# Second network: attention steps handed out in lumps instead of one by one

## The chip, the cores and the metric

The kernel runs on one NeuronCore of a Trainium2 chip. The metric is the device time of one execution in microseconds. The engines work through their own queues in order and wait for each other on semaphores: TensorE (PE) does the matmuls, VectorE (DVE), ScalarE (ACT) and GpSimd (POOL) the rest, and SyncE (SP) issues the DMAs.

## The reference

Two networks of two layers each work one after the other on x of 256 rows and 1024 columns, in float32. The change lies in the second one. Each of its layers is a swiglu with a layer norm, then a mixing block with an output projection and a layer norm, and then a second swiglu with a layer norm. Cut to the mixing block:

```python
proj = x @ w_in[l]
(h_a, b_a, c_a, uv, q, kc, vc, ksl, vsl, kw, vw, gl) = jnp.split(proj, split_points, axis=-1)
y_a = short_conv(h_a, b_a, c_a, conv_w[l])
y_b = gmlp_spatial(uv, gmlp_ln_g[l], gmlp_ln_b[l], gmlp_w[l], gmlp_b[l])
y_c = nsa_attention(q, kc, vc, ksl, vsl, kw, vw, gl, ...)
mix = jnp.concatenate([y_a, y_b, y_c], axis=-1) @ w_out[l]
x = layer_norm(ALPHA * x + mix, ln2_g[l], ln2_b[l])
```

`nsa_attention` has 8 heads in two groups and three branches: attention to 15 compressed keys, to selected blocks (with 256 rows all four blocks are selected) and to a window (which covers all rows). The last two are thus plain causal attention over 256 rows with other keys and values. Each branch is weighted by a sigmoid gate and the three are summed.

## The kernel before, in words

The weights come in float32, 1 MB at a time (a unit), by DMA. ScalarE rounds a unit to fp32r (`high`, L1785), and VectorE forms the rest, weight less rounded weight, in two halves of 1024 columns (`low`, L2009). Each product is three matmuls of such parts (L217 to L219, or L224 to L226 where the result is added to a bank that holds the residual). Three units are held ready.

The whole program is written out by a planner in Python, `script`. It makes one list of steps; each engine then goes through the list in that order and issues its share of each step. The order of the list is therefore the order of every engine's queue. Where two pieces of work are mixed, one generator yields costs in microseconds for one of them and another for the other, and `mix(a, b, share)` (L248) takes steps of b until they cost `share` times what a has cost. A generator that can't go on yet yields `IDLE`; then mix goes on with a.

In the stage of the change, a is the rest of the projections, in 28 pieces of cost 1.44: four for the values (`lin_v`), four for the second half of the queries (`lin_q(1)`), eight for the convolution (`lin_conv`), four more (`lin_conv2`) and eight of the output projection (`lin_out`). Beside the last twelve, one step of `conv` is issued after each piece: gate, two tap steps, end, split. A unit belongs to each four pieces. Behind its second piece the conversion of the unit three ahead is queued on ScalarE, and behind the third and fourth piece one half each on VectorE (`spread`).

b is `nsa` (L1249), with a share of 1.04. It has eight tasks (`task`, L1284): key set 1 or 2, row half i = 0 or 1, and head pairs jp. Each task has four steps:

- scores: eight matmuls, a mask matmul on each of two banks, two maxima on VectorE (L2118), and exponentials on ScalarE (L1855)
- scale: reciprocal, gate and two multiplies of the probabilities on VectorE (L2146 to L2155). It has no TensorE work and a cost of 0
- turn: 4 or 8 transpositions (L1496), and a copy from PSUM for each of two banks, one on ScalarE and one on VectorE (L1863, L2125)
- values: 4 or 8 matmuls (L1638). After five sums of a row half, `o_split` copies the result as fp32r on ScalarE (L1795) and its rest on VectorE (L2021)

`slots(tasks, (-1, 0, -2, -1))` (L742) staggers them: slot n issues scale of task n-1, scores of task n, values of task n-2 and turn of task n-1, and yields each cost by itself, so that mix can put pieces between them. Behind each of them one step of a second chain, `side`, is issued and yielded by itself too: what is left of the gmlp block and of the key compression (`early`: gelu, mix, tanh, split), then for each row half the attention to the compressed keys (`compressed`: scores, max, exp, mask, turn L1751, values L1760). The second `compressed` waits for the convolution.

PSUM has eight banks, handed out in the order in which they were given back. In this stage one holds the running projection, two the sums of the values and, toward the end, four the output.

Of the kernel before, what the change touches and what calls it, by code (L numbers as in the profile page):

```python
# [27 lines left out]
PART = 1.44  # L28
# [200 lines left out]
def dense(banks):  # L229
    for b in banks:  # L230
        b.dense = True
    return banks


IDLE = "idle"
# [56 lines left out]
def chain(*gens):  # L292
    for g in gens:
        if callable(g):
            g = g() or ()
        yield from g


class Plan:
# [21 lines left out]
    def add(self, kind, *args):  # L321
        self.steps.append((kind, args))
# [128 lines left out]
def script(P):  # L451
# [274 lines left out]
    def score_pair(q, k, js, i, bias, mask, rs, q_events):  # L726

        bs, ers = [PB.take() for _ in range(2)], [ER.take() for _ in range(2)]
        K = 128 * (i + 1)
        if i:  # L730
            dense(bs)
        add("score_pair", bs, [[q[64 * hh:64 * hh + 64, j, i * 128:(i + 1) * 128] for hh in range(2)] for j in js],
            [[k(hh, j)[:, 0:K] for hh in range(2)] for j in js], mask, i, q_events)
        for hh in range(2):
            if bias is not None:
                add("biased", bs[hh], 2, K, bias(hh, js, K), ers[hh], P.small(2), rs[hh])
            else:
                add("soft", bs[hh], 2, K, P.small(2), ers[hh], rs[hh])
        PB.give(*bs)
        return ers  # L740

    def slots(tasks, order):  # L742

        for n in range(len(tasks) + 2):
            for x in order:
                if 0 <= n + x < len(tasks):
                    cost = next(tasks[n + x])
                    while cost is IDLE:
                        yield IDLE
                        cost = next(tasks[n + x])  # L750
                    if cost:
                        yield cost
                elif x == 0:
                    yield PART

    def turned(ers, i):

        K, T = 128 * (i + 1), i + 1
        ets = []
        for er in ers:  # L760
            tb, et = PB.take(), ET.take()
            add("weigh", tb, [er.ap[:, n * K + mt * 128:n * K + mt * 128 + 128] for n in range(2) for mt in range(T)], er, ("scaled", er.n), et, P.flip)
            P.flip = not P.flip
            PB.give(tb)
            ER.give(er)
            ets.append(et)
        return ets
# [90 lines left out]
    def first(l, o, now, nxt):  # L858
# [95 lines left out]
        def ca_attention():  # L954
# [8 lines left out]
            def task(i, jp):  # L963
                js, T = (2 * jp, 2 * jp + 1), i + 1
                rs, rc = P.small(4), P.small(4)
                ers = score_pair(q1, K, js, i, bias, None, [[rs[:, 2 * hh + n:2 * hh + n + 1] for n in range(2)] for hh in range(2)],
                                 [("q ca", l), ("k ca", l)])
                yield 1.45 + 0.95 * i
                add("scale", ers, rs, rc, None, 128 * T)
                yield 0  # L970
                ets = turned(ers, i)
                yield 0.44 * T
                if jp == 0:
                    obs[i], = dense([PB.take()])
                ob = obs[i]
                outs = [(hh, ob.ap[64 * hh:64 * hh + 64, j * 128:(j + 1) * 128], v1[:, mt, (2 * j + hh) * 64:(2 * j + hh + 1) * 64],
                         ets[hh].ap[:, (n * T + mt) * 128:(n * T + mt + 1) * 128]) for n, j in enumerate(js) for mt in range(T) for hh in range(2)]
                add("values_t", ob, ets, outs, jp == 0, jp == 1, [("v ca", l, 1)], [("ca read", l)] if i else [])
                ET.give(*ets)
                if jp == 1:  # L980
                    add("o_split", ob, range(4), (), (), [O2[:, z, 0:4, i * 128:(i + 1) * 128] for z in (0, 1)],
                        [("ht read", ("first", l - 1), 10)] if l else [], [("o2 ca", l)], 1.0)
                    PB.give(ob)
                yield 0.45 * T
# [105 lines left out]
    def second(l, o, nxt):  # L1090
# [158 lines left out]
        def nsa():  # L1249
            obs, sums = {}, [0, 0]  # L1250

            def part(i, kind, *args):

                if not sums[i]:
                    obs[i], = dense([PB.take()])
                ob = obs[i]
                add(kind, ob, *args[:2], sums[i] == 0, sums[i] == 4, *args[2:])
                sums[i] += 1
                if sums[i] == 5:
                    add("o_split", ob, range(4), (), (), [O1[:, z, 4:8, i * 128:(i + 1) * 128] for z in (0, 1)], [o1_before], [("o1 nsa", l, i)], 1.0 / ALPHA)  # L1260
                    PB.give(ob)

            def compressed(i):
                er, mx, rs = ER.take(), P.small(8), P.small(8)
                bs = [PB.take() for _ in range(2)]
                add("cmp_scores", l, i, bs, er, kcs)
                PB.give(*bs)
                yield 0.5
                add("cmp_max", l, i, er, mx)
                yield 0.5  # L1270
                add("cmp_exp", l, i, er)
                yield 0.5
                add("cmp_mask", l, i, er, rs, gts)
                yield 0.9
                tb, et = PB.take(), ET.take()
                add("cmp_turn", l, i, er, tb, et)
                PB.give(tb)
                ER.give(er)
                yield 0.3
                part(i, "cmp_values", l, et)  # L1280
                ET.give(et)
                yield 1.0

            def task(i, bno, jp):  # L1284

                js, T = (2 * jp, 2 * jp + 1), i + 1
                rs, rc = P.small(4), P.small(4)

                def K(hh, j):
                    return KS[64 * hh:64 * hh + 64, bno - 1, :]  # L1290
                if jp:
                    yield from at.until("q")
                ers = score_pair(Q, K, js, i, None, causalb, [[rs[:, 2 * hh + n:2 * hh + n + 1] for n in range(2)] for hh in range(2)],
                                 [("q nsa", l, jp), ("k nsa", l), "masks"])
                yield 1.1 + 0.5 * i
                gate = gts[:, 24 * i:24 * i + 24].rearrange("p (g j b) -> p g j b", g=2, j=4)[:, :, 2 * jp:2 * jp + 2, bno]
                add("scale", ers, rs, rc, (("gates", l), gate), 128 * T)
                yield 0
                ets = turned(ers, i)
                yield 0.44 * T  # L1300
                yield from at.until("v")
                outs = [(hh, lambda ob, hh=hh: ob.ap[64 * hh:64 * hh + 64, jp * 256:(jp + 1) * 256].rearrange("p (n q) -> p n q", n=2),
                         VS[:, mt, (bno - 1) * 128 + hh * 64:(bno - 1) * 128 + (hh + 1) * 64],
                         ets[hh].ap[:, 0:2 * T * 128].rearrange("p (n t q) -> p n t q", n=2, t=T)[:, :, mt, :]) for mt in range(T) for hh in range(2)]
                part(i, "values_t", ets, outs, [("v nsa", l)], [("win read", l)])
                ET.give(*ets)
                yield 0.45 * T
            main = slots([task(i, bno, jp) for jp in range(2) for i in range(2) for bno in (1, 2)], (-1, 0, -2, -1))
            side = chain(lambda: early, at.until("q"), lambda: compressed(0), at.until("conv"), lambda: compressed(1))
            for cost in main:  # L1310
                if cost is IDLE:
                    yield IDLE
                    continue
                yield cost
                x = next(side, IDLE)
                if x is not IDLE:
                    yield x
            yield from side

        at = Line()  # L1320
# [8 lines left out]
        early = weave([gmlp(0), gmlp(1), both()], 3)  # L1329
        mix(chain(lin_cmp(), lin_k(), lin_gates(), lin_q(0)), early, 0.6, False)  # L1330
        steps = nsa()
        acc = [[], []]

# [1052 lines left out]
def build(nc, I, out_ap):  # L2386
    with ExitStack() as ctx:
# [28 lines left out]
        sems = {k: ctx.enter_context(nc.semaphore("s_" + k)) for k in SEMS}  # L2416
        P = Plan(m, I)
        script(P)
        steps = P.settled()
        T = Events()  # L2420
# [41 lines left out]
```

## Time and profile before

| | us |
|---|---|
| median of 3 runs | 1994.32 (1994.09 to 1995.76) |
| the profiled execution | 1995.39 |
| its span | 1993.5 |
| TensorE busy | 1974.0 (99%), 13856 matmuls |
| VectorE busy | 1254.2 (63%) |
| ScalarE busy | 904.8 (45%) |
| GpSimd busy | 99.3 (5%) |
| DMA queue, share of 16 engines | 59.0% |

A busy TensorE isn't one at its peak: matmuls overlap, and the end of each is modelled. What counts is the distance between the starts. The granted clock of TensorE is full (1.00) over nearly the whole span. The stage of the change lies at about 1220 to 1295 us for the first layer and at 1716 to 1790 us for the second.

### The profile page before, as it was taken

What the parts mean: (1) busy time and instruction counts of PE and PEld (TensorE: products, weight loads), DVE (VectorE), ACT (ScalarE), POOL (GpSimd) and SP (SyncE); (2) the same over time, 40 slices, a digit from 0 to 9 for tenths busy, and PEclk for the clock granted to TensorE, in tenths of its full rate; (3) what the DMA queues carried; (4) which work ended last, traced back from release to release, by engine and by line L of the source; (5) the groups of instructions that cost most, each with busy time, mean ns of one, the idle gap of its engine ahead of it and who ended that gap; (6) DMA issues with size and microseconds to landing.
All of it is one profiled execution on the core that took longest, in us unless ns stands there. A gap on an engine that the chain in (4) does not pass through costs nothing.

```text
span 1993.5 us, 31852 instructions
## 1 busy us (share of the span) xinstructions
PE 1974.0 (99%) x13856; PEld 1801.5 (90%) x13856; DVE 1254.2 (63%) x1785; ACT 904.8 (45%) x1202; POOL 99.3 (5%) x84
## 2 busy tenths in 40 slices
PE   8999999999999999999999999999999999999998
PEld 7888999999888999999999989799999998979997
DVE  6566656665656766655565567765566556776555
ACT  4445444444445544444444445444444444444442
POOL 0000001000100000100100020010010002001000
PEclk9999999999999999999999999999999999999999
DMA  8444466666544455796666646368657665646663
GB/s 289 165 146 148 170 211 189 199 210 191 171 167 149 141 177 197 196 264 181 180 203 188 189 151 173 106 194 259 190 169 212 189 187 148 176 106 195 187 189 106
DMA packets 421412, 361.84 MB, mean 182 GB/s; under 512 B 29392, under 2 KB 361496, under 8 KB 421272
## 3 DMA queue, kind: packets, MB, share of 16 engines
q1 hardware_dynamic: 421272, 359.80, 59.0%
q8 instruction: 109, 1.79, 0.4%
q14 instruction: 31, 0.25, 0.0%
HBM read 358.72 MB, written 1.05 MB: 180 GB/s over the span
## 4 chain that ended last, share of the span: by engine, by line
PE 95%; DVE 4%; ACT 1%; issue 0%; DMA 0%; DVEq 0%; SPq 0%
PE ps L217 22%; PE ps L218 22%; PE ps L219 22%; PE ps L224 8%; PE ps L226 8%; PE ps L225 8%; PE ps L1496 2%; PE ps L1604 1%; DVE hl L2009 1%; PE ps L1638 1%; DVE small L2114 0%; PE ps L1609 0%; ACT hl L1785 0%; PE ps L1676 0%; DVE er L2112 0%; DVE er L2155 0%
## 5 line engine op out<-in xcount | busy, mean ns | idle before, releaser
L2009 DVE TENSOR_TENSOR hl<-raw,hl 128x1024 fp32r<-128x1024 f32 (+1 forms) x532 | 722.6, 1391 | 387.0 <-ACT hl L1785 385.9
L217 PE MATMUL ps<-xt,hl 128*128 128x256 f32 (+1 forms) x2672 | 754.2, 282 | 0.0
L218 PE MATMUL ps<-xt,hl 128*128 128x256 f32 (+1 forms) x2672 | 746.2, 279 | 0.0
L219 PE MATMUL ps<-xt,hl 128*128 128x256 f32 (+1 forms) x2672 | 745.8, 279 | 0.0
L1785 ACT ACTIVATE hl<-raw 128x2048 fp32r<-128x2048 f32 (+1 forms) x337 | 613.7, 1829 | 217.9 <-PE ps L226 157.5
L217 PEld LDWEIGHTS ps<-xt,hl 128*128 128x128 f32 (+1 forms) x2672 | 500.9, 187 | 5.4 <-issue 2.3
L218 PEld LDWEIGHTS ps<-xt,hl 128*128 128x128 f32 (+1 forms) x2672 | 501.1, 188 | 3.1
L219 PEld LDWEIGHTS ps<-xt,hl 128*128 128x128 f32 (+1 forms) x2672 | 500.8, 187 | 0.2
L224 PE MATMUL ps<-hl,o 128*128 128x512 f32 x656 | 261.3, 398 | 0.0
L226 PE MATMUL ps<-hl,o 128*128 128x512 f32 x656 | 259.0, 395 | 0.0
L225 PE MATMUL ps<-hl,o 128*128 128x512 f32 x656 | 258.8, 395 | 0.0
L217 PE MATMUL ps<-hl,xt 128*128 128x512 f32 (+1 forms) x576 | 207.7, 361 | 1.3 <-DVE hl L2009 1.3
L219 PE MATMUL ps<-hl,xt 128*128 128x512 f32 (+1 forms) x576 | 202.6, 352 | 0.0
L218 PE MATMUL ps<-hl,xt 128*128 128x512 f32 (+1 forms) x576 | 202.5, 352 | 0.0
L1833 ACT ACTIVATE th<-ps 128x256 f32<-128x256 f32 x132 | 50.6, 384 | 329.3 <-PE ps L219 329.3
L226 PEld LDWEIGHTS ps<-hl,o 128*128 128x128 f32 x656 | 123.5, 188 | 28.8
L224 PEld LDWEIGHTS ps<-hl,o 128*128 128x128 f32 x656 | 123.5, 188 | 27.3 <-issue 1.5
L225 PEld LDWEIGHTS ps<-hl,o 128*128 128x128 f32 x656 | 123.7, 189 | 25.5
L217 PEld LDWEIGHTS ps<-hl,xt 128*128 128x128 f32 x576 | 108.7, 189 | 19.2 <-DVE hl L2009 2.3
L219 PEld LDWEIGHTS ps<-hl,xt 128*128 128x128 f32 x576 | 108.6, 189 | 16.1
L218 PEld LDWEIGHTS ps<-hl,xt 128*128 128x128 f32 x576 | 108.9, 189 | 14.6
L2092 DVE SCALAR_TENSOR_TENSOR tm<-th,ps 128x256 f32<-128x256 f32 x132 | 55.5, 421 | 99.3 <-ACT th L1833 95.3
(197 smaller groups left out, 1578.9 us busy)
## 6 DMA issues: line engine op xcount, KB each, us to landing
raw<-in_w_in SPq DMA_DIRECT2D x83, 1024.0 KB, 5.0
raw<-in_w_ffn_in SPq DMA_DIRECT2D x88, 512.0 KB, 5.1
raw<-in_ffn_gate SPq DMA_DIRECT2D x88, 512.0 KB, 3.9
raw<-in_ffn_up SPq DMA_DIRECT2D x88, 512.0 KB, 5.2
raw<-in_ffn_down SPq DMA_DIRECT2D x44, 1024.0 KB, 5.1
raw<-in_w_ffn_out SPq DMA_DIRECT2D x22, 1024.0 KB, 5.0
raw<-in_w_out SPq DMA_DIRECT2D x24, 512.0 KB, 4.7
raw<-in_w_branch_a SPq DMA_DIRECT2D x8, 1024.0 KB, 5.0
```

Source lines behind the costliest of these rows:

```text
L217: e.matmul(out, l[0], r[0], start=start, stop=False)
L218: e.matmul(out, l[0], r[1], start=False, stop=False)
L219: return e.matmul(out, l[1], r[0], start=False, stop=stop)
L224: e.matmul(out, l[0], r[0], start=False, stop=True, skip_group_check=True)
L225: e.matmul(out, l[0], r[1], start=False, stop=True, skip_group_check=True)
L226: return e.matmul(out, l[1], r[0], start=False, stop=True, skip_group_check=True)
L1496: ins = e.transpose(b.ap[:, k * 128:(k + 1) * 128], x, ident)
L1604: ins = e.matmul(b.ap[:, n * K:(n + 1) * K], qs[n][hh], ks[n][hh], start=n == 0, stop=mask is None and n == 1)
L1785: e.activation(m["hl"][:, k % NHL, 0, c], m["raw"][:, k % NRAW, c], ACT.Copy).then_inc(s.high.up(*([("high", k, h)] if parts == 2 else [(" ...
L1833: e.activation(tha, ga, ACT.Tanh, scale=0.5).then_inc(done.up(th.full), 1)
L2009: e.tensor_tensor(lo[:, c], m["raw"][:, k % NRAW, 0:n][:, c], hi[:, c].bitcast(F), ALU.subtract).then_inc(s.low.up(("low", k), *([("low", ...
L2092: e.scalar_tensor_tensor(tma, tha, 1.0, ga, ALU.add, ALU.mult).then_inc(done.up(th.free), 1)
```

## The change

`slots` is replaced by a new function `lumps` in `nsa`. It goes through the same tasks in the same order, but adds the costs of a slot's steps up and yields them once. Mix can therefore place pieces only between slots. Where a task yields `IDLE`, what has been added up so far is yielded first. Behind each lump two steps of `side` are issued, and their cost is added to the lump's before it is yielded, where there was one step behind each attention step. Nothing is computed otherwise, and no instruction is added or left out.

```diff
+    def lumps(tasks, order):
+
+        for n in range(len(tasks) + 2):
+            lump = 0
+            for x in order:
+                if 0 <= n + x < len(tasks):
+                    cost = next(tasks[n + x])
+                    while cost is IDLE:
+                        if lump:
+                            yield lump
+                            lump = 0
+                        yield IDLE
+                        cost = next(tasks[n + x])
+                    lump += cost
+                elif x == 0:
+                    yield lump + PART
+                    lump = 0
+            if lump:
+                yield lump
...
-            main = slots([task(i, bno, jp) for jp in range(2) for i in range(2) for bno in (1, 2)], (-1, 0, -2, -1))
+            main = lumps([task(i, bno, jp) for jp in range(2) for i in range(2) for bno in (1, 2)], (-1, 0, -2, -1))
             side = chain(lambda: early, at.until("q"), lambda: compressed(0), at.until("conv"), lambda: compressed(1))
             for cost in main:
                 if cost is IDLE:
                     yield IDLE
                     continue
+                for _ in range(2):
+                    x = next(side, IDLE)
+                    if x is not IDLE:
+                        cost += x
                 yield cost
-                x = next(side, IDLE)
-                if x is not IDLE:
-                    yield x
             yield from side
```

## Rows read from the trace of the kernel before

**Rows 1.** Waits of TensorE over the span: who, for whom, us in total, times, longest.

```profile
PE ps L1638 <- DVE et L2125: 2.3, 2, 1.2
PE ps L1760 <- DVE et L2373: 1.6, 2, 0.8
PE ps L1496 <- DVE er L2155: 1.4, 2, 0.7
```

**Rows 2.** Busy us of each engine in the first layer's stage, clock, DMA share, GB/s.

```profile
1213.00:1300.00 87.00, 84.38 (x658) 70.67 (x654) 62.41 (x134) 41.33 (x100) 1.22 (x2) 1.00 0.46 132
```

**Rows 3.** Timeline of TensorE, a piece between steps: start, us, engine, line, what.

```profile
1232.03 0.36 PE L217 MATMUL ps<-xt,hl 128*128 128x256 f32 x1
1232.22 0.28 PE L218 MATMUL ps<-xt,hl 128*128 128x256 f32 x1
...
1234.80 0.27 PE L219 MATMUL ps<-xt,hl 128*128 128x256 f32 x1
1235.00 0.65 PE L1638 MATMUL ps<-et,v 128*64 128x256 f32 x4
```

**Rows 4.** Timeline of TensorE, steps of the first slots.

```profile
1222.78 0.39 PE L1609 MATMUL ps<-maskb 128*128 128x256 bf16 x2
1223.10 0.24 PE L1684 MATMUL ps<-cst,tm 30*128 30x30 f32 x2
1223.27 0.38 PE L217 MATMUL ps<-hl,xt 128*128 128x256 f32 x1
...
1227.18 1.00 PE L1733 MATMUL ps<-sg,v 128*128 128x64 f32 x8
1228.02 0.61 PE L1496 MATMUL ps<-cst,er 128*128 128x128 f32 x4
```

**Rows 5.** Timeline of ScalarE and VectorE around the first turn.

```profile
1225.37 1.93 ACT L1785 ACTIVATE hl<-raw 128x2048 fp32r<-128x2048 f32 x1
...
1226.01 0.76 DVE L2155 TENSOR_TENSOR er<-er,small 128x256 f32<-128x256 f32 x2
...
1227.35 1.22 DVE L2009 TENSOR_TENSOR hl<-raw,hl 128x1024 fp32r<-128x1024 f32 x1
1228.48 0.86 DVE L2338 SCALAR_TENSOR_TENSOR sg<-ps,small,sg 128x64 f32<-128x64 f32 x4
```

**Rows 6.** Timeline of VectorE, the last slots.

```profile
1268.64 1.29 DVE L2118 TENSOR_REDUCE small<-ps 128x2 f32<-128x512 f32 x2
...
1269.84 0.35 DVE L2294 TENSOR_SCALAR tm<-zb,small 128x256 f32<-128x256 f32 x1
...
1271.15 1.22 DVE L2009 TENSOR_TENSOR hl<-raw,hl 128x1024 fp32r<-128x1024 f32 x1
...
1272.86 0.69 DVE L2021 SCALAR_TENSOR_TENSOR o<-ps,o 128x512 fp32r<-128x512 f32 x1 [0.49 <-ACT o L1795]
...
1273.46 0.68 DVE L2125 COPY et<-ps 128x512 f32<-128x512 f32 x1
...
1276.50 0.17 DVE L2146 RECIPROCAL small<-small 128x4 f32<-128x4 f32 x1
...
1276.91 1.29 DVE L2155 TENSOR_TENSOR er<-er,small 128x512 f32<-128x512 f32 x2
```

**Rows 7.** Timeline of ScalarE, four exponentials of a task and a split.

```profile
1233.50 0.48 ACT L1855 ACTIVATE er<-ps,small 128x256 f32<-128x256 f32 x1 [2.82 <-DVE small L2118]
...
1235.32 0.26 ACT L1909 ACTIVATE small<-small 128x60 f32<-128x60 f32 x1
...
1237.26 0.39 ACT L1795 ACTIVATE o<-ps 128x256 fp32r<-128x256 f32 x1
```

**Rows 8.** TensorE's first full and last matmuls, and the last clock change (columns as rows 2).

```profile
10.82 0.63 PE L218 MATMUL ps<-hl,xt 128*128 128x512 f32 x1
...
1986.43 0.39 PE L226 MATMUL ps<-hl,o 128*128 128x512 f32 x1
...
1989.50:1990.00 0.50, 0.00 (x0) 0.00 (x0) 0.40 (x2) 0.00 (x0) 0.00 (x0) 0.70 0.00 0
```

## The prediction

> **What bounds the kernel now.** I read the page's shares first (the table above): TensorE is busy 1974.0 of 1993.5 us, so almost every microsecond is either matmul work or the step from one matmul to the next, and an edit that only reorders can save no more than idle time and the cost of changing from one kind of work to another. Then the waits of TensorE: apart from the start there are three kinds, each with two occurrences, one per layer of the second network, 5.3 us together [rows 1]. All lie in the stage that the diff touches: 84.38 of 87 us busy, so 2.6 us idle per layer [rows 2]. Last the timeline of that stage, engine by engine, to see what each later queue is doing when TensorE arrives.
>
> **The order before and after.** Both follow from the costs in the code: `mix` hands out attention steps until they have cost 1.04 times what the projection pieces (1.44 each) have. Adding this up by hand for 28 pieces, the old order comes out as the trace shows it. The new one, with t0 to t7 for the tasks: lump n holds scale t(n-1), scores t(n), values t(n-2), turn t(n-1), then two side steps. The lumps 0 to 8 stand behind pieces 1, 3, 5, 7, 10, 12, 15, 18 and 20, lump 9 is cut in two behind 22 and 23, and the last compressed pair stands behind 25, as before. (Lump 8 is cut too, but both parts fall behind piece 20.) The pieces begin again behind attention work 12 times, where it was 23.
>
> **What is removed: 11 re-entries.** The first matmul of a piece takes 0.19 us to the second, against 0.117 between later ones, and work on 64 rows begins 0.20 behind the last one [rows 3]: 0.08 going in and 0.08 coming out, 0.16 for each, 1.8 us per layer. Something comes back: a score pair ends in a bf16 mask matmul, behind which an fp32 instruction starts only 0.32 later [rows 4], where a piece starts after 0.15. Seven lumps now have fp32 work there: 7 x 0.17 = 1.2 us, if the row, which is for a small transposition, holds for values and turns too. So between 0.6 and 1.8; I take the middle, -1.2 us per layer.
>
> **What is added: waits inside the lumps.** The turn of t(n-1) needs its rows scaled by VectorE. In the old order pieces stood between scores, values and turn; now they don't, while VectorE and ScalarE still have the same things queued, in particular the conversions of the weights (ScalarE 1.93 us, then VectorE in halves of 1.13) [rows 5]. I walk each lump with the durations of the rows.
>
> Lump 1: piece 2 starts 0.84 us later than the old 1223.27, because a mix of eight matmuls moves ahead of it [rows 4]; pieces 2 and 3 take 2.98, scores 0.97. TensorE is at the turn of t0 at 1228.06. ScalarE's conversion still starts at 1225.37 and lasts 1.93, so VectorE's first half still starts at 1227.35 and gives it free at 1228.48. In the old order the scaling of t0 was done before it, at 1226.01 [rows 5]; now it is queued behind it, as it comes behind piece 3. With 0.41 for the reciprocal and the small multiply [rows 6] and 0.42 for the first scaled tile (the pair is recorded with 0.76) the turn can start at 1229.3: a wait of 1.25, and 0.1 for the second tile. Price 1.35.
>
> Lump 3: from the end of the scores of t2 TensorE has values 0.58, a turn 0.44, two splits 0.5, two pieces 2.98, scores 1.39, values 0.58: 6.5 us. The other chain: maximum 0.7, four exponentials 1.82 [rows 7], a copy and two splits at some 0.4 [rows 7], a conversion 1.93, VectorE's half 1.13, scaling 0.41 + 0.69: 7.85. Price 1.35, and 0.15 for the second tile: 1.5.
>
> Lump 6: the turn of the compressed probabilities and their product are the two side steps of one lump, with no piece between. That is the place where the old order waits 0.8 us at its end [rows 1]; the first of the two pairs was covered by a piece. VectorE is some 0.25 later here, since maximum and copy of two tasks are queued first. Price 1.05.
>
> Lump 8, the largest. VectorE in the old order needed 1276.91 + 0.69 (its time for 128x512) - 1268.64 = 9.0 us from the first maximum of t7 to its first scaled tile [rows 6], and TensorE waited 1.2 and 0.7. New queue, from that same maximum: two maxima 1.2; then the low half of `o_split`, which used to stand behind a tap step and a conversion. It can't start before ScalarE has finished four exponentials (0.7 + 1.82) and its own half (128x512; by the 0.39 for 256 and 1.93 for 2048 columns I estimate 0.61): 3.2. From there split 0.6, copy 0.6, taps 1.3, conversion 1.13, taps 1.3, conversion 1.13, scaling 0.41 + 0.69: 10.4 us. TensorE's cover in the same time: values 0.58, turn 0.86, pieces 19 and 20 2.98, values 1.01: 5.4, since piece 21 now stands behind the turn. A wait of 5.0 and 0.15 for the second tile, where there were 1.9 before: +3.3.
>
> Elsewhere the walk leaves room: the turns of lumps 2, 4, 5, 6 and 7 find their tiles scaled 0.8 to 2.5 us before, the banks of the new order are free when taken (nearest: the compressed scores, in lump 4, take a bank whose exponential ends 0.6 us before), and rings, loads and units are asked for at the same pieces as before. The last pair waits 0.8 as before. The DMAs aren't moved; of SP's and POOL's queues nothing is passed.
>
> **Sum** per layer: 1.35 + 1.5 + 1.05 + 3.3 = 7.2, less 1.2: +6.0 us. The two layers have the same steps, and the waits come in twos [rows 1]: +12.0. What follows is paced by TensorE, so nothing is won back. The profiled run took 1995.4 with a span of 1993.5, 1.1 above the median 1994.3; the difference is added to the median: 2006.3. With each wait 0.5 us shorter and the switches at 1.8 it is 2001, with each 0.5 longer and the switches at 0.6 it is 2011.5.
>
> **Rules of the skill.** TensorE's granted clock is 1.00 in this stage [rows 2], so nothing can be won on it. The Trainium skill (Perfetto Trace Analysis, Matmul Optimizations) says that it is "important that matmuls execute back-to-back in batches", because the engine scales with its use; that speaks for lumps, and would give a gain only if the clock were low somewhere.
>
> **Rivals.**
> *A. The clock falls in the long wait.* At the kernel's end the last matmul starts at 1986.43, and between 1989.5 and 1990 the granted clock is 0.70 on average, a change from the upper level (2.4 GHz) to the lower (1.2 GHz) some 3 us after the last matmul [rows 8]. The new 5 us wait is longer. The first matmuls of the kernel, after a 5.3 us wait, are recorded with 0.63 us [rows 8] where full speed gives 0.40, for about seven of them and 16 transposes before. Price: 7 x 0.2 for the matmuls alone, up to 3.2 with the transposes, for each fall; both layers give 2009 to 2012.5. The Trainium skill (TensorE: Matmul & The Clock Gate, Part 1: The HAM clock gate) says the same: an idle engine is throttled, and activity releases it.
> *B. Only the tail pays.* If VectorE is a microsecond ahead of my walk in lumps 1, 3 and 6, three waits go: +3.3 - 1.2 = 2.1 per layer, 1998.5. For it: VectorE is busy only 62.4 of 87 us in the stage [rows 2]. Against: the conversion sets its time, not its load.
> *C. Faster.* One mechanism: the queue in front of t7's scaling. If the `o_split` half and the taps overlap with ScalarE so that the scaled tile comes within 7 us of the first maximum, the wait there falls to the old 1.9, and if the other lumps are covered as in B, the 11 re-entries remain: -1.8 per layer, 1990.7. It decides at 5.4 + 1.9 us; the rows put it at 10.4, and in the old order at 9.0.
> *D. The lumps are no lumps.* Where a task or the side yields idle, a lump is cut. By the costs this happens in 8 and 9 only. If it happened everywhere, the time would be as before, within 0.2%.
>
> **Chances.** Forecast 0.50 (2001 to 2009), A 0.20 (2007 to 2012.5), B 0.15, C 0.07, D and other things that cancel 0.08. A measurement can tell about 0.2% (4 us) from no change: faster 0.07; within 0.2%, D and a third of B, 0.13; slower 0.80. The range, 1998.5 to 2012, holds the forecast, A and most of B.
>
> **What would show it.** Of the changed kernel: TensorE's waits in this stage should have turns waiting for the scaled tile three times per layer (about 1.3, 1.4 and 5.0), and the product of the compressed probabilities twice (about 1.1 and 0.8); busy time of the stage longer by some 6 us at equal work; 12 re-entries of the 0.32 or 0.20 kind in place of 23. ScalarE's half of `o_split` should come straight behind t7's exponentials with VectorE idle before the low half. If the long wait is under 3 us, the tail's walk is wrong; if matmuls behind it are recorded with over 0.28 us for 256 columns, A holds; if lumps 1 and 3 don't wait, B does.

## The result and the profile after

The changed kernel takes 2012.96 us (median of 5 runs, 2011.57 to 2013.64) where the kernel before takes 1994.32: a ratio of 1.0089 with an interval of 1.0078 to 1.0099, or 18.6 us more. The sign was forecast; the size was not, and the time lies above the range. The profiled execution took 2013.23 us with a span of 2011.4.

The page of the kernel after: busy time of the engines, and the shares of the chain that ended last.

```profile
PE 1979.2 (98%) x13856; PEld 1804.0 (90%) x13856; DVE 1255.1 (62%) x1785; ACT 904.7 (45%) x1202; POOL 99.4 (5%) x84
...
PE 92%; DVE 5%; ACT 2%; issue 1%; DMA 0%; DVEq 0%; SPq 0%
```

The same 13856 matmuls, as they must be. The kernel before had 95% of its chain on TensorE and 4% on VectorE. So the new time lies in waits for VectorE, and TensorE's busy time has risen too, by 5.2 us at equal work. Those are two effects, and the forecast had only the first.

All lines behind `slots` are moved by 21: the turn is L1517 (was L1496), the values L1659, the mask L1630, scale L2167 to L2176, the conversion L1806 on ScalarE and L2030 on VectorE. Waits of TensorE in the kernel after over the whole span (who, for whom, us in total, times, longest):

```profile
PE ps L1517 <- DVE er L2176: 14.2, 6, 4.7
PE ps L1781 <- DVE et L2394: 3.6, 4, 1.0
```

Beside [rows 1]: the wait of the values has fallen from 1.2 to 0.1 us, turns wait three times per layer in place of once, and the compressed product waits twice in place of once. Timeline of TensorE in the first layer (start, us, engine, line, what; in brackets the idle time before it), the two early turns:

```profile
1229.54 0.64 PE L1517 MATMUL ps<-cst,er 128*128 128x128 f32 x3 [1.21 <-DVE er L2176]
...
1242.94 1.26 PE L1517 MATMUL ps<-cst,er 128*128 128x128 f32 x8 [1.17 <-DVE er L2176]
```

And the tail of the same layer, VectorE, ScalarE and TensorE together:

```profile
1273.13 1.29 DVE L2139 TENSOR_REDUCE small<-ps 128x2 f32<-128x512 f32 x2 [1.77 <-PE ps L1630]
...
1275.67 0.61 ACT L1816 ACTIVATE o<-ps 128x512 fp32r<-128x512 f32 x1
...
1276.31 0.69 DVE L2042 SCALAR_TENSOR_TENSOR o<-ps,o 128x512 fp32r<-128x512 f32 x1 [1.89 <-ACT o L1816]
...
1277.75 1.08 PE L1659 MATMUL ps<-et,v 128*64 128x256 f32 x8
...
1278.82 1.22 DVE L2030 TENSOR_TENSOR hl<-raw,hl 128x1024 fp32r<-128x1024 f32 x1
...
1281.26 1.22 DVE L2030 TENSOR_TENSOR hl<-raw,hl 128x1024 fp32r<-128x1024 f32 x1
...
1282.80 1.29 DVE L2176 TENSOR_TENSOR er<-er,small 128x512 f32<-128x512 f32 x2
...
1283.55 1.97 PE L1517 MATMUL ps<-cst,er 128*128 128x128 f32 x8 [4.71 <-DVE er L2176]
1285.17 0.78 PE L224 MATMUL ps<-hl,o 128*128 128x512 f32 x1
1285.74 0.63 PE L225 MATMUL ps<-hl,o 128*128 128x512 f32 x1
1286.17 0.63 PE L226 MATMUL ps<-hl,o 128*128 128x512 f32 x1
...
1287.20 0.40 PE L226 MATMUL ps<-hl,o 128*128 128x512 f32 x1
```

This is the queue of the forecast, item by item: maxima at 1273.13, the low half of `o_split` after 1.89 us of idle VectorE, two tap steps with a conversion behind each, then the scaling of t7. The first scaled tile is done 10.4 us after the first maximum (1282.80 + 0.69 - 1273.13). Behind the wait, the eight transpositions are recorded with 1.97 us where the turn at 1242.94 took 1.26, and matmuls of 512 columns start 0.43 apart and are recorded with 0.63, until the spacing is 0.23 and the record 0.40 again.

Busy time of each engine around the two long waits of the kernel after (columns as rows 2: PE, weight load, DVE, ACT, POOL, granted clock, DMA share, GB/s):

```profile
1281.00:1283.00 2.00, 0.00 (x0) 0.00 (x0) 1.93 (x5) 0.00 (x0) 0.00 (x0) 1.00 0.00 0
1283.00:1285.00 2.00, 1.46 (x7) 1.46 (x8) 1.09 (x2) 0.30 (x1) 0.00 (x0) 0.62 0.59 169
1285.00:1287.00 2.00, 2.00 (x8) 1.66 (x7) 1.28 (x2) 0.43 (x2) 0.00 (x0) 0.52 1.18 317
1287.00:1289.00 2.00, 2.00 (x11) 1.37 (x9) 0.69 (x1) 2.00 (x2) 0.00 (x0) 1.00 0.16 38
...
1788.00:1790.00 2.00, 2.00 (x10) 1.90 (x9) 0.54 (x2) 0.60 (x1) 0.00 (x0) 0.50 1.07 312
1790.00:1792.00 2.00, 2.00 (x7) 1.52 (x6) 1.30 (x3) 1.06 (x2) 0.00 (x0) 0.50 0.76 195
```

The clock falls from the upper level (2.4 GHz) to the lower (1.2 GHz): rival A's case. In the first layer it falls as the wait ends, at about 1283.5, and is back up at about 1287. In the second it falls at about 1785.3, in the middle of a wait that ends at 1787.62, and stays low for nearly 7 us, until 1792; some 4.5 us of that are work.

**Where the 18.6 us are.** From the first piece of the stage to the first transposition of the layer norm that ends it, the kernel before needs 82.27 us in both layers, the kernel after 90.85 and 91.37: 8.58 + 9.10 = 17.7 us, of 17.9 by which the spans of the two profiled executions differ. The remaining 0.9 is within the spread of the runs of either. Net of TensorE's recorded waits (2.63 us per layer before, 8.87 and 8.84 after) the stage takes 79.64 before and 81.98 and 82.52 after. These two numbers, *waits* and *net*, are the measure for all that follows. Waits under 0.15 us are not counted and stay in the net time, and so does what a low clock costs.

### The profile page after: what moved, and what is told of

It reads as the page before. It is cut to its first block, busy times and chain, and to the rows that moved or that the text cites. A ratio compares the mean times of both kernels' runs of the same rounds, so it can differ in the third digit from the quotient of the medians.

```text
span 2011.4 us, 31840 instructions
## 1 busy us (share of the span) xinstructions
PE 1979.2 (98%) x13856; PEld 1804.0 (90%) x13856; DVE 1255.1 (62%) x1785; ACT 904.7 (45%) x1202; POOL 99.4 (5%) x84
## 3 DMA queue, kind: packets, MB, share of 16 engines
HBM read 358.72 MB, written 1.05 MB: 179 GB/s over the span
## 4 chain that ended last, share of the span: by engine, by line
PE 92%; DVE 5%; ACT 2%; issue 1%; DMA 0%; DVEq 0%; SPq 0%
PE ps L217 21%; PE ps L218 21%; PE ps L219 21%; PE ps L224 8%; PE ps L226 8%; PE ps L225 8%; PE ps L1517 2%; DVE hl L2030 1%; ACT hl L1806 1%; PE ps L1625 1%; ACT er L1876 1%; PE ps L1659 1%; DVE er L2176 0%; DVE small L2135 0%; PE ps L1697 0%
## 5 line engine op out<-in xcount | busy, mean ns | idle before, releaser
L2030 DVE TENSOR_TENSOR hl<-raw,hl 128x1024 fp32r<-128x1024 f32 (+1 forms) x532 | 722.4, 1390 | 389.4 <-ACT hl L1806 388.4
L1806 ACT ACTIVATE hl<-raw 128x2048 fp32r<-128x2048 f32 (+1 forms) x337 | 613.8, 1829 | 222.5 <-PE ps L226 159.0
```

Source lines behind the costliest of these rows:

```text
L1806: e.activation(m["hl"][:, k % NHL, 0, c], m["raw"][:, k % NRAW, c], ACT.Copy).then_inc(s.high.up(*([("high", k, h)] if parts == 2 else [(" ...
L2030: e.tensor_tensor(lo[:, c], m["raw"][:, k % NRAW, 0:n][:, c], hi[:, c].bitcast(F), ALU.subtract).then_inc(s.low.up(("low", k), *([("low", ...
```

## The experiments

Where an expectation names a theory by a letter, K is the one with the clock's fall in it, and Q the one that puts the waits down to the order of VectorE's queue. The kernel before had 1995.78, 1994.67 and 1995.13 us on the chips of the experiments. "Entries" are the places where pieces begin again behind other work. The net time of e2 holds some 4.1 us of added work. Chips differ by up to 1.5 us, so differences between runs of different chips are taken from the stages of their traces.

| kernel | us | ratio to before | interval | first layer: length | waits | net | entries |
|---|---|---|---|---|---|---|---|
| before | 1994.32 | 1 | | 82.27 | 2.63 | 79.64 | 23 |
| after | 2012.96 | 1.0089 | 1.0078 to 1.0099 | 90.85 | 8.87 | 81.98 | 12 |
| e1 | 2003.31 | 1.0043 | 1.0030 to 1.0055 | 86.65 | 6.00 | 80.65 | 14 |
| e2 | 2009.73 | 1.0070 | 1.0056 to 1.0084 | 89.45 | 4.81 | 84.64 | 12 |
| e3 | 2010.01 | 1.0072 | 1.0059 to 1.0085 | 89.42 | 7.59 | 81.83 | 12 |
| e4 | 2015.52 | 1.0099 | 1.0086 to 1.0113 | 92.26 | 8.77 | 83.49 | 11 |
| e6 | 1999.14 | 1.0020 | 1.0011 to 1.0030 | 84.12 | 3.63 | 80.49 | 14 |
| e7 | 2005.75 | 1.0056 | 1.0042 to 1.0070 | 87.28 | 6.48 | 80.80 | 18 |
| e8 | 1994.12 | 0.9996 | 0.9987 to 1.0004 | 81.55 | 1.47 | 80.08 | 23 |
| e9 | 1991.78 | 0.9986 | 0.9977 to 0.9994 | 80.49 | 0.68 | 79.81 | 24 |
| e10 | 2022.96 | 1.0138 | 1.0122 to 1.0154 | 98.20 | 11.60 | 86.60 | 12 |
| e11 | 1993.95 | 0.9995 | 0.9986 to 1.0004 | 82.00 | 1.67 | 80.33 | 15 |
| e12 | 1992.12 | 0.9983 | 0.9974 to 0.9992 | 80.49 | 0.69 | 79.80 | 24 |

### The tail alone: e1_tail_apart

From slot 7 on the steps are handed out one by one, as the kernel before does; slots 0 to 6 stay lumps.

```diff
+            if n == 7:
+                P.apart = True
+            if P.apart:
+                for x in order:
+                    ...
+                        if cost:
+                            yield cost
+                    ...
+                continue
```

> The changed kernel, but from slot 7 on the steps are handed out one by one, as before. Theory K: of the 18.6 us some 3.6 are two falls of the TensorE clock behind the 4.7 us waits for the scaled tiles of t7, 6 are those waits themselves, and the rest are the waits in lumps 1, 3 and 6 with nothing won by fewer re-entries. Then the tail waits are 1.2 and 0.7 again, the clock stays at 1.00, and the time is 2013.0 - 3.6 - 2 x 3.0 = 2003.4. Rival R: a lower clock costs nothing here and the excess over my sum lies in the lumps themselves; then only the waits go, 2007.

Measured 2003.31. The two stages are shorter than in the kernel after by 4.20 and 4.72 us, 8.9 together (the medians, of two chips, differ by 9.65). So half of the loss lay in the tail, the clock's share with it. The waits of t0, t2 and the first compressed product are still there (1.2, 1.2 and 1.0), the clock is 1.00 throughout the stage. With the waits taken off, the stage is still 1.0 us longer than before although pieces begin again 9 times less. That is the first sign that the 1.2 us for the re-entries are not there.

### The clock alone: e2_warm

In front of t7's turn TensorE does 36 transpositions of the identity into the bank that the turn then fills, so that it is busy in the long wait, with nothing else changed.

```diff
+        for _ in range(warm):
+            e.transpose(tb.ap[:, 0:128], ident, ident)
```

> The changed kernel with 36 extra transpositions of the identity on TensorE (0.105 us each, 3.8 us) into the bank that t7's turn takes, placed in the 4.7 us wait; their result is overwritten. K: the turn starts at the same time, but the clock doesn't fall: 2013.0 - 3.6 = 2009.4, the first layer shorter by 1.5 and the second by 2.1. R: 2013 or a little more.

Timeline and window of e2_warm, first layer:

```profile
1278.69 4.15 PE L1638 MATMUL ps<-cst 128*128 128x128 f32 x36
...
1283.48 1.26 PE L1518 MATMUL ps<-cst,er 128*128 128x128 f32 x8 [0.64 <-DVE er L2179]
1284.49 0.48 PE L224 MATMUL ps<-hl,o 128*128 128x512 f32 x1
...
1283.00:1287.00 4.00, 3.52 (x19) 2.90 (x20) 2.55 (x5) 1.51 (x3) 0.00 (x0) 1.00 0.86 239
```

The turn starts where it did (1283.48 against 1283.55), since VectorE sets it. But the clock is 1.00, the turn takes 1.26 again instead of 1.97, and the stage is shorter by 1.40 us in the first layer and 1.90 in the second. So the fall costs 3.3 us, worked out as two stages; the medians say 3.2. In the first layer 0.61 of the 1.40 lie in the eight transpositions (1.62 against 1.01 to the next start) and 0.79 in the twelve matmuls behind them (3.76 against 2.97); in the second it is 0.61 and 1.28, since the clock comes back later. It is the measured price of rival A. It also separates two effects of one wait: the turn came no earlier, and the kernel was faster all the same.

### Taking one item out of VectorE's queue: e3_split_late

The first `o_split` is issued behind the second tap step instead of in front of t7's copy.

```diff
-                    add("o_split", ob, range(4), ...)
-                    PB.give(ob)
+                    def split(ob=ob):
+                        add("o_split", ob, range(4), ...)
+                        PB.give(ob)
+                    ...
+                if c:
+                    comp["split"]()
```

> The changed kernel, but the first o_split is issued behind the second tap step, so that VectorE doesn't stand idle for ScalarE's half (1.9 us in the changed kernel). If the order of VectorE's queue sets the long wait, it shrinks from 4.7 to about 3.4: -2.6 us in all, and -3.6 more if the clock then stays: 2006.8, or up to 2010.4 if it falls in both layers. If only the missing TensorE cover sets it, it stays 4.7 and the time 2013.

Waits of TensorE in e3_split_late over the span, and one window of it:

```profile
PE ps L1524 <- DVE er L2183: 11.6, 6, 3.4
...
1281.00:1283.00 2.00, 2.00 (x10) 1.76 (x10) 0.79 (x2) 0.60 (x1) 0.00 (x0) 0.53 0.92 271
```

The wait fell from 4.71 to 3.4, as forecast from the durations of the queue: it is the sum of what stands in front of the scaling (Q). The clock fell all the same in both layers, so 3.4 us of idle TensorE were enough here.

### Covering the wait with pieces: e4_piece_back

Lump 8 is cut in front of t7's turn, so that pieces 21 and 22 stand before it.

```diff
+                    if n == 8 and x == -2:
+                        yield lump + PART
+                        lump = 0
```

> The changed kernel, but lump 8 is cut between the values of t6 and the turn of t7, so that pieces 21 and 22 stand between them (3.0 us of cover, VectorE's queue as in the changed kernel up to t7's scaling). K: the wait falls to 1.7, the clock stays: 2013.0 - 6.2 - 3.6 + 0.4 = 2003.6. R: 2007.2.

It missed by 12 us: 2015.52. Waits, timeline of ScalarE and TensorE, and windows of e4_piece_back:

```profile
PE ps L1520 <- DVE er L2179: 8.2, 6, 1.7
PE ps L1768 <- ACT et L1887: 5.8, 2, 2.9
...
1285.31 1.89 ACT L1809 ACTIVATE hl<-raw 128x2048 fp32r<-128x2048 f32 x1
...
1287.11 0.58 ACT L1887 ACTIVATE et<-ps 128x512 f32<-128x512 f32 x1
...
1285.00:1287.00 2.00, 0.00 (x0) 0.00 (x0) 1.29 (x2) 2.00 (x2) 0.00 (x0) 0.97 1.17 321
1287.00:1289.00 2.00, 1.26 (x12) 1.26 (x14) 0.00 (x0) 1.70 (x4) 0.00 (x0) 0.50 0.28 67
...
1291.00:1293.00 2.00, 2.00 (x6) 1.60 (x5) 1.90 (x7) 0.00 (x0) 0.00 (x0) 0.50 0.00 0
```

The wait for the scaled tile is 1.7, as forecast. But a new one of 2.89 us stands behind it: the compressed scores take the bank of t7's turn, and ScalarE's copy of that bank (1287.11) is queued behind a weight conversion (1285.31, 1.89 us). I had walked VectorE's queue and not ScalarE's. The other lesson is the clock: no single wait is over 2.9 us, and yet it goes from 1.00 to 0.50 at about 1287 and stays there until after 1293. It falls 2.0 us into the wait of 2.9; the wait of 1.7 had ended 1.25 us before that one began (1283.60, and 1284.85). The waits of 1.2 in the same stage brought none. What the two waits each contribute was not taken apart.

### The early waits: e6_low_late

e1, and VectorE's two conversion halves are queued one piece later each.

```diff
+        self.let_low()
+        if self.late and piece in (2, 3):
+            self.held = piece
+            return
...
+    def let_low(self):
+        if self.held is not None:
+            self.add("need_low", self.held - 2)
+        self.held = None
```

> The kernel of e1 (lumps up to slot 6, the tail one by one), but VectorE's two halves of each weight conversion are queued one piece later, so that in lumps 1 and 3 the scaling stands ahead of the half. Theory Q (the place of the conversion in VectorE's queue makes the waits of 1.2 us in these lumps): both go, -6.0 us against e1, ratio 1.0013 to the kernel before. Rival D (VectorE is loaded too much when TensorE comes in lumps, wherever the conversion stands): at least half of the two waits stays, ratio 1.003 or more.

Waits of TensorE in e6_low_late in its first layer (1213 to 1310), and the timeline of the first scaling and the first turn:

```profile
PE ps L1815 <- DVE et L2428: 1.8, 2, 1.0
PE ps L1693 <- DVE et L2180: 1.1, 1, 1.1
PE ps L1551 <- DVE er L2210: 0.7, 1, 0.7
...
1225.56 0.76 DVE L2210 TENSOR_TENSOR er<-er,small 128x256 f32<-128x256 f32 x2
...
1226.99 0.39 PE L1664 MATMUL ps<-maskb 128*128 128x256 bf16 x2
1227.22 0.60 PE L1551 MATMUL ps<-cst,er 128*128 128x128 f32 x4
```

Both early waits are gone: the scaling of t0 is done before the conversion (1225.56; 1228.97 in the kernel after), and the turn follows the mask without a stop. (Its stage begins 0.95 us earlier than that of the kernel after.) Q holds. Some 4 us remain to the kernel before. Half of it are waits (3.63 against 2.63 per layer), the other half is the net time, 80.49 against 79.64, at 9 entries less. Here it can be read start by start, with the clock at 1.00 throughout:

- The pieces together take 52.05 us against 53.08, waits left out: -1.02, or 0.11 per entry saved and not the 0.16 of the forecast. A piece takes about 1.50 in front of work on 128 rows and 128 columns (1.59 in front of one turn) and 1.58 to 1.62 in front of scores (64 rows) and values (64 columns), and only the dearer kind costs more than a piece among pieces (1.40 to 1.50).
- The mask pairs up to the next start take 2.31 against 1.36: +0.95.
- The turns, with those of the compressed probabilities, take 0.57 more. What counts most is what follows a turn. Eight transpositions behind values take 0.85 up to a piece and 1.02 up to small fp32 matmuls; the difference is in the step from the last of them, 0.03 to the piece and 0.20 to the others. Standing behind values in place of a piece adds 0.06 (0.85 against 0.79).
- The second compressed scores take 1.34 against 1.00: +0.34.
- All the rest together: +0.02.

That is the whole +0.86. The step behind a turn, before and in e6:

```profile
1243.44 1.09 PE L1496 MATMUL ps<-cst,er 128*128 128x128 f32 x8
1244.29 0.37 PE L217 MATMUL ps<-xt,hl 128*128 128x256 f32 x1
...
1247.12 1.09 PE L1551 MATMUL ps<-cst,er 128*128 128x128 f32 x8
1248.14 0.62 PE L1799 MATMUL ps<-small,q 64*128 64x15 f32 x8
```

The 0.34 of the compressed scores isn't the lumps' doing. e8 and e9 below, which have no lumps but the later conversion halves, show it too (1.33), and e1, which has lumps and not the later halves, does not (1.00). Before, and VectorE and TensorE in e6:

```profile
1280.25 1.07 PE L1744 MATMUL ps<-small,q 64*128 64x15 f32 x16
...
1279.38 1.22 DVE L2064 TENSOR_TENSOR hl<-raw,hl 128x1024 fp32r<-128x1024 f32 x1
1280.51 0.69 DVE L2180 COPY et<-ps 128x512 f32<-128x512 f32 x1
1280.90 1.41 PE L1799 MATMUL ps<-small,q 64*128 64x15 f32 x16
```

A conversion half now stands in front of VectorE's copy of t7's turn, and in e4 these scores waited for the other copy of that turn. That they wait a little for this one here, without the trace recording it as idle time, is likely and was not tested. Without it, e6's lumps cost 0.52 us net per layer.

The mask is seen best in timelines of TensorE. After, where fp32 work of 64 columns follows it:

```profile
1235.00 0.39 PE L1630 MATMUL ps<-maskb 128*128 128x256 bf16 x2
1235.32 0.65 PE L1659 MATMUL ps<-et,v 128*64 128x256 f32 x4
```

0.32 us from the start of the pair to that of the values, in each of the lumps with values; from a mask pair to a piece the kernel before needs 0.15. It is the same step of 0.17 as behind a turn. In front of the first turn of e6 (fence above) it is 0.23.

### Giving the side steps back: e7_side_apart

e1, with each of the two side steps yielded by itself.

```diff
+                yield cost
                 for _ in range(2):
                     x = next(side, IDLE)
                     if x is not IDLE:
-                        cost += x
-                yield cost
+                        yield x
```

> The kernel of e1, but the two side steps behind each lump are handed out by themselves. By the plan's costs the compressed turn and its product still stand together, but behind piece 17 and with no maximum and copy ahead of them: their wait shrinks from 1.0 to 0.8. There are 18 re-entries in place of 16 or so. If joining the side steps costs little, as I think, the ratio to the kernel before stays at 1.004; if it were a main part of the loss, 1.002 or less.

2005.75, no gain over e1. The compressed product waits 0.8 in place of 1.0, but the lumps stand at other pieces. The turns of t0 and t2 wait 1.20 and 1.27 as in e1, and another turn, at 1264.33, now waits 0.63 in each layer. In the trace a conversion half (VectorE, 1262.31 to 1263.4) stands right in front of the scaling that it needs (1263.85): the shifted lump meets another conversion, as in lump 1. That was read from the trace and not tested by itself.

### The kernel before, with the same cures: e8 and e9

e8 gives the kernel before e6's later conversion halves (that edit is shown above), and the first output banks are seeded one piece later. e9 is e8 with the cost of the first compressed turn of the second row half raised, so that mix puts piece 26 between it and its product.

```diff
-                if n == 1:
+                if n == 2:
...
-                yield 0.3
+                yield 1.8 if i else 0.3
```

> The kernel before, with the conversion halves queued one piece later and the first two seeds of the output banks one piece later (behind the second tap step), so that ScalarE's half of o_split comes 1.1 us sooner. If VectorE's and ScalarE's queues set the tail waits of the kernel before (1.2 and 0.7 us per layer), these shrink or go: -2.4 to -3.8 us, 1990.5 to 1992. If they are set by work that can't move, it stays at 1994.3.

> The kernel of e8, and in the second row half piece 26 stands between the compressed turn and its product. The last wait (0.8 us per layer) goes: -1.6 us against e8, 1989 to 1990.5. If the o_split behind it then comes too late for the output projection, TensorE waits there instead and nothing is won against e8.

e8: the wait of the values falls from 1.16 to 0.12, the counted waits from 2.63 to 1.47, but the net time rises by 0.44, and 1994.12 is no measurable change. The 0.44 are that 0.12 and the second compressed scores, 1.33 in place of 1.00. It is the later seeds that take the wait of the values away: e6, with the later halves alone, still has 1.15. So the later halves take no wait away in this kernel, and cost some 0.3 us per layer. e9: 1991.78, and repeated as e12_tail_again 1992.12 (ratios 0.9986 and 0.9983, both intervals under 1). Its waits over the span:

```profile
PE ps L1509 <- DVE er L2168: 1.4, 2, 0.7
```

Only t7's turn still waits over 0.15 us in the stage. This is the fastest version, some 0.15% under the kernel before and 1% under the kernel after, and it has *more* entries (24), not fewer.

> The kernel of e9 again, beside e11: 1991.8, ratio 0.9986 to the kernel before.

### Scores last: e10_scores_last

To avoid fp32 work behind the mask, the order in a lump becomes scale, values, turn, scores, with the side steps in front; else e6. The side steps' cost is added to the next lump's, and the first lump starts with a cost of 2.0, which shifts it by a piece.

```diff
-            main = lumps([...], (-1, 0, -2, -1))
+            main = lumps([...], (-1, -2, -1, 0))
```

> The kernel of e6, but in each lump up to slot 6 the order is side steps, scale, values, turn, scores, so that a projection piece follows the mask matmul. If the bf16 mask matmul with an fp32 instruction behind it is what eats the saving of the lumps, the mask pairs take 0.15 us to the next start in place of 0.32 in seven places, and the stage without its waits is 1.0 us per layer shorter than e6's 80.5. The turns have less cover (values only), and the tail comes a piece later, so waits may come back; I expect 1997 to 2000 for the time. If the loss inside the lumps lies elsewhere, the stage without waits stays at 80.5.

A plain miss: 2022.96. TensorE's timeline around one mask, its waits and one window in e10_scores_last:

```profile
1222.83 0.39 PE L1668 MATMUL ps<-maskb 128*128 128x256 bf16 x2
1222.98 0.37 PE L217 MATMUL ps<-hl,xt 128*128 128x256 f32 x1
...
PE ps L1555 <- DVE er L2214: 18.7, 12, 2.6
...
1228.00:1230.00 2.00, 0.91 (x4) 0.72 (x4) 1.21 (x6) 0.21 (x1) 0.00 (x0) 0.62 0.00 0
```

The term that it was made for is confirmed: a piece follows all eight mask pairs of a layer, six of them after 0.15, and two, at the lower clock, after 0.26. But the scores of t(n) had been the cover of the scaling of t(n-1). Without them turns wait 12 times for a scaled tile, and the clock falls three times in the first layer and twice in the second, with no wait over 2.6. The first fall of the first layer comes 1.2 us into a wait of 1.82. A wait of 2.15 is followed by a fall in the first layer (1248.96) and by none in the second (1758.78, the clock 1.00 from 1743.9 to 1784.9), at the same place of the same program. The shift also changed the order of the tail, so this run tells only the 0.15 and what lost cover costs, not what a lump without the mask's price would bring.

### Lumps with all cures: e11_lumps_tail

e6 with e9's two edits: lumps up to slot 6, and the best tail found.

> The kernel of e6 with e9's tail (seeds later, piece 26 between the last compressed turn and its product). If lumps gain nothing by themselves once their waits are gone, it is slower than e12 by the wait in lump 6 (2.1 us for both layers) and the 0.85 us per layer that e6 has without waits: 1991.8 + 3.8 = 1995.6. If fewer re-entries win anything, it is under 1993.

1993.95, against 1992.12 and 1991.78 for the same cures without lumps. In the first layer it still has 1.67 us of waits against 0.69, and 80.33 net against 79.80, with 15 entries against 24. Of the 1.5 us per layer by which the stages differ, 0.98 are the wait of the compressed product, the one wait of the lumps that this cure leaves, and 0.53 are net. So fewer entries win nothing, and the lumps lose by both.

## Why the prediction was wrong in size and right in sign

**The order and the walks: right.** The pieces begin again 12 times, lump by lump as written out. The waits, forecast against measured: t0's turn 1.25 and 1.21, t2's 1.35 and 1.17, the first compressed product 1.05 and 1.00, t7's turn 5.0 and 4.71, the last pair as before. With the second tiles (0.14 and 0.17) and the 0.11 that the values still wait they come to 7.2 forecast and 6.66 measured, net of the old waits. Walking VectorE's queue from the rows of before, in list order, gave every new wait within 0.3 us.

**The clock: the first step that failed.** Rival A had the case, at a chance of 0.20, and the forecast left its price out. The rows spoke for it: [rows 8] put a fall some 3 us after the last matmul, and the forecast wait was 5.0. I had no row of a fall inside the kernel, and took that for a reason to leave it out, where the nearest row should have decided. e2 gives the price: 1.40 and 1.90 us, at the low end of the 1.4 to 3.2 each of rival A, since it was 8 transpositions and the matmuls behind them that were slow, not 16. The Trainium skill (TensorE: Matmul & The Clock Gate, Part 1: The HAM clock gate) says that an idle TensorE is throttled; the trace agrees, with 0.50 granted in both layers.

**The re-entries: the term that was mis-sized.** Forecast -1.2 us per layer, within 0.6 to 1.8 of gain. Measured: the stages are longer by 8.58 and 9.10 us; less 6.66 of waits and less the clock's 1.40 and 1.90, +0.52 and +0.54 remain. Not even the sign was in the bounds. e2, whose clock is full, shows the parts against the kernel before: the pieces are 1.52 us shorter (0.14 for each of the 11 entries, forecast 0.16 and 1.8 in all), the mask pairs 1.29 longer (forecast 1.2), and the turns, second tiles left out, 0.57 longer; the rest adds some 0.2. So two steps of the term were wrong. It took the middle between 1.8 and 0.6, where the mask's price stood in full, and it put the turns at nothing. The kernel before had a row for them: four transpositions in front of scores take 0.53 (1261.35), in front of a piece 0.41 (1265.26). I bounded this term only on the side of a gain, though the rows that I read reached only one kind of transition. The same size comes out twice more: e6 has +0.52 once the 0.34 of the later halves is taken off, and e11 against e12, with 9 entries less, +0.53. (What the prediction calls work on 64 rows in [rows 3] is work on 128 rows and 64 columns; the spacing that it reads there is right.)

**The sum.** Forecast 12.0; with the clock +3.3, the re-entries 1.72 + 1.74 = +3.5, and the waits 0.54 x 2 = -1.1 it is 17.7, the difference of the two stages. Rival A, priced at up to 2012.5, came within 0.5 us of the median, but by too high a price for the clock, which stood in for the re-entries.

**The other rivals.** B (only the tail pays) fell: lumps 1 and 3 wait 1.21 and 1.17. It described what e6's edit brings about. C (faster) fell at its own point: the scaled tile came at 10.4 us after the first maximum, where 10.4 was forecast and 7 was the condition. D fell.

**A rule weighed.** The Trainium skill (Perfetto Trace Analysis, Matmul Optimizations) wants matmuls back-to-back in batches. Here TensorE was busy 99% of the span before, at the full clock, so the rule had nothing to give. The lumps made the attention work contiguous and the whole 0.9% slower, by the waits that they opened; the clock was low only after.

## What to carry to other kernels

Independent matmul work between two steps of a chain is the cover for the other engines' part of that chain. Before gathering steps, walk each engine's queue in list order (ScalarE's as well as VectorE's, weight conversions included) and price the wait in front of each step that loses its cover; here the walks along VectorE's queue were good to 0.3 us. Where a walk gives waits of the size with which the clock fell here (1.8 to 4.7 us, the shorter ones not every time), add the price of the fall; and where a gain is a sum of small transitions, bound it below zero too, unless the trace shows each new pair of neighbours.

## What the runs showed of the hardware

- TensorE's granted clock fell in e4 with no wait over 2.9 us, and in e10 with none over 2.6, there once 1.2 us into a wait of 1.82; a wait of 2.15 was followed by a fall in one layer of e10 and not in the other. In the stages of e1, e6 and e9, with waits up to 1.2 us, it stayed at 1.00. In the kernel after it was low for some 3.5 us in one layer and for nearly 7 us in the other. What decides between the two was not tried.
- Transpositions of the identity kept the clock up: 36 of them in 4.15 us per layer gained 3.3 us over the two stages of the kernel after, though their result is overwritten.
- From the start of a bf16 mask pair to the next start it is 0.32 us where values of 64 columns follow and 0.15 where a piece follows; from the last of eight fp32 transpositions it is 0.20 us to small fp32 matmuls and 0.03 to a piece. Whether the type, the rows or the loading of the weights makes this was not taken apart.
